# A two-layer encoder on one core: the opening stage in a new order, with its own ring for the modulation weights

## The chip, the cores and the metric

The kernel runs on one core of a Trainium2 chip. TensorE (PE) multiplies matrices into PSUM, VectorE (DVE), ScalarE (ACT) and GpSimd (POOL) work on elements, SyncE (SP) issues most transfers from HBM; each engine takes its instructions in order and waits on semaphores. The metric is the device time of one execution in microseconds (us), as the median of several runs. Less is better.

## What is computed

```python
for i in range(2):
    shift, scale, gate = split(silu(c) @ w_mod[i] + b_mod[i])      # each D = 1024
    h = rmsnorm(x, norm_g[i]) * (1 + scale) + shift                # x: 512 x 1024
    if i == 0:     # layer A: short convolution
        z, bg, cg, xh = split(h @ a_w_in)                          # each E = 2048
        y = bg * conv3(cg * xh) * silu(z);   y = y @ a_w_out
    else:          # layer B: spatial gating
        z, u, v = split(h @ b_w_in);  u, v = gelu(u), layernorm(gelu(v))
        y = u * (w_s @ v + b_s) * silu(z);   y = y @ b_w_out
    x = x + gate * y
out = rmsnorm(x, final_g)
```

All in fp32. The kernel holds x transposed, 128 channels a tile (8 tiles, KD) by 512 positions.

## The kernel before

To keep fp32 accuracy, every operand of a large product is cut in two: an upper part that ScalarE writes as fp32r (`h_hi`, `w_hi`), and the rest that VectorE subtracts (`h_lo`, `w_lo`). A product is then three matmuls, hi*hi, hi*lo and lo*hi. Layer A works on E = 2048 in eight pairs of 256 columns. Pair 0 is done in the opening in the plain way; pairs 1 to 7 are done in a loop by a scheme with seven products of 256 columns (Q1 to Q7) for each group of weights (four groups a pair, `g` = 0 to 3; `product`, L890 to L892), for which VectorE first makes sums of h (`s_f`, cut into `s_hi` and `s_lo`) and of weights (`wt`, by `t_sums`), lower parts of a weight block (`b11_low`) and of the sums (`t_low`), and ScalarE copies each bank's partial result between products (`copy_p`, L545).

The opening, up to that loop, does this. Eight tiles of x arrive in four transfers and ScalarE squares them; VectorE adds the squares up with GpSimd's help; TensorE sums over channels (L829), GpSimd takes the power -1/2 (L417), and a product with diagonals spreads the result (`p_rstd`, L805, "broadcast"). In parallel the modulation of layer A is needed: shift and scale of h are sums over 1024 rows of `w_mod`, which arrive as 16 slots of 512 KB, s0 to s3, four slots for each pair of h tiles (kp = 0 to 3). VectorE multiplies each 512 columns by silu(c) and adds them up (`start_tile`, L1153 and L1156, 32 steps in all), TensorE sums over partitions with four one-column products (`start_columns`, L774), VectorE makes `amp` and `mod`, and ScalarE makes the two tiles of h and their upper parts (L471, L475). Two of the steps of kp = 0 are done by TensorE from the raw slot with silu(c) as one moving column (`direct_columns`, L819). GpSimd does the scalings of x by the norm for tiles 2 to 7 (L429) and the lower part of every odd h tile (L425). TensorE then has, for each kp, 24 matmuls for cg and xh (L845) and 12 for z (`p_pair`), and at the end 48 for bg.

The order is written out by hand in each engine's block. All slots of the opening, modulation and weights (0 to 7), go through one ring `raw` of four slots in the order of `START_ORDER`; SyncE waits on `consumed`, which VectorE raises when it is done with a slot. `keep_clock` (L767) issues matmuls on constants whose result nobody reads, 15, 3 and 12 of them.

## Time and profile before

| | us |
|---|---|
| median of 3 runs | 846.73 |
| lowest, highest | 845.67, 846.97 |
| profiled execution | 845.46 |
| its span in the trace | 843.4 |
| TensorE busy | 819.3 |
| VectorE busy | 627.2 |
| ScalarE busy | 381.7 |
| GpSimd busy | 52.4 |

The profiled execution is one run with its own time; 2.1 us of it lie outside the span that the trace covers. Times in the trace are microseconds from the start of the span. Busy shares are averages over stages with different limits, so the stretches are to be read one by one. A line number is the line of the kernel before; a helper's line stands for all its calls.

### The profile page before, as it was taken

What the parts mean: (1) busy time and instruction counts of PE and PEld (TensorE: products, weight loads), DVE (VectorE), ACT (ScalarE), POOL (GpSimd) and SP (SyncE); (2) the same over time, 40 slices, a digit from 0 to 9 for tenths busy, and PEclk for the clock granted to TensorE, in tenths of its full rate; (3) what the DMA queues carried; (4) which work ended last, traced back from release to release, by engine and by line L of the source; (5) the groups of instructions that cost most, each with busy time, mean ns of one, the idle gap of its engine ahead of it and who ended that gap; (6) DMA issues with size and microseconds to landing.
All of it is one profiled execution on the core that took longest, in us unless ns stands there. A gap on an engine that the chain in (4) does not pass through costs nothing.

```text
span 843.4 us, 14120 instructions
## 1 busy us (share of the span) xinstructions
PE 819.3 (97%) x5026; PEld 736.7 (87%) x5026; DVE 627.2 (74%) x966; ACT 381.7 (45%) x514; POOL 52.4 (6%) x56
## 2 busy tenths in 40 slices
PE   5899899999999999999999999999999999999996
PEld 4778899999999999987889888888888888888896
DVE  4989989898989999898653664477776667667534
ACT  3346566666665665553323832244344444422210
POOL 2510000001000000000000100000000000000000
PEclk9899999999999999999999999999999999999999
DMA  7674466666565666578422232222222222174203
GB/s 269 231 252 151 125 181 196 182 188 173 175 187 173 187 174 181 177 281 300 158 76 75 76 125 99 99 82 93 99 75 87 87 94 80 50 273 149 78 1 100
DMA packets 35467, 123.13 MB, mean 146 GB/s; under 512 B 3824, under 2 KB 6000, under 8 KB 35440
## 3 DMA queue, kind: packets, MB, share of 16 engines
q1 hardware_dynamic: 31120, 107.05, 35.7%
q0 software_dynamic: 4032, 14.68, 9.2%
q10 hardware_dynamic: 288, 1.05, 0.3%
q8 instruction: 16, 0.26, 0.1%
q14 instruction: 11, 0.09, 0.0%
HBM read 105.99 MB, written 2.10 MB: 128 GB/s over the span
## 4 chain that ended last, share of the span: by engine, by line
PE 88%; DVE 8%; issue 1%; DMA 1%; ACT 1%; SPq 0%; DVEq 0%
PE pp L751 14%; PE pp L753 14%; PE pp L752 14%; PE pp L890 7%; PE pp L891 7%; PE pp L892 7%; PE p_aux L892 4%; PE p_aux L890 4%; PE p_aux L891 4%; PE pp L1026 3%; PE pp L1027 3%; PE pp L1028 3%; DVE acc_s L1153 3%; PE p_aux L1079 1%; DVE w_lo_s L1133 1%
## 5 line engine op out<-in xcount | busy, mean ns | idle before, releaser
L456 ACT ACTIVATE w_hi<-raw 128x1024 fp32r<-128x1024 f32 x77 | 81.5, 1060 | 183.9 <-PE pp L753 117.3
L1133 DVE TENSOR_TENSOR w_lo<-raw,w_hi 128x1024 fp32r<-128x1024 f32 x80 | 97.5, 1222 | 70.4 <-ACT w_hi L456 70.0
L751 PE MATMUL pp<-y_hi,w_hi 128*128 128x512 f32 (+1 forms) x320 | 114.6, 358 | 0.7 <-DVE y_lo L1407 0.4
L752 PE MATMUL pp<-y_lo,w_hi 128*128 128x512 f32 (+1 forms) x320 | 111.1, 347 | 0.0
L753 PE MATMUL pp<-y_hi,w_lo 128*128 128x512 f32 (+1 forms) x320 | 111.1, 347 | 0.0
L751 PE MATMUL pp<-h_hi,w_hi 128*128 128x512 f32 x256 | 100.2, 391 | 0.0
L753 PE MATMUL pp<-h_hi,w_lo 128*128 128x512 f32 x256 | 99.7, 389 | 0.0
L752 PE MATMUL pp<-h_lo,w_hi 128*128 128x512 f32 x256 | 99.6, 389 | 0.0
L891 PE MATMUL pp<-h_lo,wh 128*128 128x256 f32 x280 | 79.2, 283 | 0.0
L892 PE MATMUL pp<-h_hi,wl 128*128 128x256 f32 x280 | 79.2, 283 | 0.0
L890 PE MATMUL pp<-h_hi,wh 128*128 128x256 f32 x280 | 79.2, 283 | 0.0
L751 PEld LDWEIGHTS pp<-y_hi,w_hi 128*128 128x128 f32 x320 | 60.6, 189 | 8.0 <-issue 1.5
L753 PEld LDWEIGHTS pp<-y_hi,w_lo 128*128 128x128 f32 x320 | 60.5, 189 | 7.6
L1347 DVE TENSOR_TENSOR wl<-wt,wh 128x1024 fp32r<-128x1024 f32 x56 | 66.5, 1219 | 0.1
L890 PE MATMUL pp<-s_hi,wh 128*128 128x256 f32 x224 | 63.5, 283 | 2.8 <-ACT pc L545 2.8
L752 PEld LDWEIGHTS pp<-y_lo,w_hi 128*128 128x128 f32 x320 | 60.6, 189 | 6.3
L538 ACT ACTIVATE wh<-wt 128x1024 fp32r<-128x1024 f32 x56 | 59.0, 1054 | 14.4 <-DVE wt L1328 8.4
L891 PE MATMUL pp<-s_lo,wh 128*128 128x256 f32 x224 | 63.4, 283 | 0.0
L892 PE MATMUL pp<-s_hi,wl 128*128 128x256 f32 x224 | 63.4, 283 | 0.0
L892 PE MATMUL p_aux<-s_hi,wl 128*128 128x256 f32 x224 | 63.4, 283 | 0.0
L890 PE MATMUL p_aux<-s_hi,wh 128*128 128x256 f32 x224 | 63.4, 283 | 0.0
L891 PE MATMUL p_aux<-s_lo,wh 128*128 128x256 f32 x224 | 63.4, 283 | 0.0
(187 smaller groups left out, 1918.5 us busy)
## 6 DMA issues: line engine op xcount, KB each, us to landing
raw<-in_stream SPq DMA_DIRECT2D x160, 512.0 KB, 3.4
wl<-raw POOLq DMA_DIRECT2D x28, 512.0 KB, 4.5
raw_l<-in_stream SPq DMA_DIRECT2D x18, 512.0 KB, 4.7
raw_m<-in_stream SPq DMA_DIRECT2D x14, 512.0 KB, 3.3
x_s<-in_xt SPq DMA_DIRECT2D x4, 512.0 KB, 6.6
x<-in_xt SPq DMA_DIRECT2D x4, 512.0 KB, 5.8
out_t<-x SPq DMA_DIRECT2D x8, 256.0 KB, 2.3
rs_bc<-in_wst ACTq DMA_DIRECT2D x1, 512.0 KB, 7.7
```

The lines of the kernel that those rows point to most:

```text
L456: act.activation(to[:, slot[0], :], raw[:, slot[1], :], ACT.Copy).then_inc(hi_cut, 1)
L538: act.activation(wh[g % 2][:, at], wt[g % 2][:, at], ACT.Copy).then_inc(t_hi_cut, 1)
L751: pe.matmul(out, hi, rhs_hi(kt), start=first and n == 0, stop=False)
L752: pe.matmul(out, hi, rhs_lo(kt), start=False, stop=False)
L753: mm = pe.matmul(out, lo, rhs_hi(kt), start=False, stop=last and n == len(kts) - 1)
L890: pe.matmul(out, hi, hi_of(k), start=fresh and k == 0, stop=False, skip_group_check=not fresh)
L891: pe.matmul(out, hi, lo_of(k), start=False, stop=False, skip_group_check=not fresh)
L892: mm = pe.matmul(out, lo, hi_of(k), start=False, stop=k == 3, skip_group_check=not fresh)
L1026: pe.matmul(v_bank(st)[:, :], left_hi, right_hi, start=kt == 0, stop=False)
L1027: pe.matmul(v_bank(st)[:, :], left_hi, right_lo, start=False, stop=False)
L1133: dve.tensor_tensor(lo[:, slot[0], :], raw[:, slot[1], :], f32(hi[:, slot[0], :]), ALU.subtract).then_inc(consumed, 1)
L1347: dve.tensor_tensor(wl[par][:, part], wt[par][:, part], f32(wh[par][:, part]), ALU.subtract).then_inc(t_cut, 1)
```

## The change

The change touches the opening only. What it does:

- The slots s0 to s3 get a ring of their own, `raw_s`, with 12 places; the weights keep the ring of four. SyncE issues all of them in the old order, and waits only for the third set (its places lie over the squares) and for the fourth set (it uses places of s0). The small constants `cols` are issued by ScalarE.
- TensorE takes the first two slots of s0 and the first of s1 straight from the raw slot, six steps of the 32 instead of two. It does so with silu(c) repeated 120 times as the moving operand (`silu_w`), so each product has 120 columns, of which one is read.
- GpSimd no longer adds squares, scales tiles or makes lower parts of h. VectorE does these.
- `keep_clock` is 6 and 2 instead of 15, 3 and 12.
- The order of VectorE, ScalarE and TensorE up to the loop is new; the middle tap of pair 0's convolution goes to ScalarE.

TensorE from its start to the first matmuls of layer A. Before (`ssum` are the sums of squares, `work` the diagonals, `acc_s` the modulation sums):

```order
L767 MATMUL pp<-ones 128x128 x15
L829 MATMUL p_aux<-ones,ssum 128x1 x4
L819 MATMUL p_aux<-silu_c,raw 128x1 x8
L767 MATMUL pp<-ones 128x128 x3
L805 MATMUL p_aux<-work,ones 128x512
L774 MATMUL p_aux<-ones,acc_s 128x1 x4
L767 MATMUL pp<-ones 128x128 x12
L845 MATMUL pp<-h_hi,w_hi_s 128x512 x4
```

and with the change:

```order
L796 MATMUL pp<-ones 128x128 x6
L841 MATMUL p_aux<-silu_w,raw_s 128x120 x8
L854 MATMUL p_aux<-ones,ssum 128x1 x4
L841 MATMUL p_aux<-silu_w,raw_s 128x120 x8
L831 MATMUL p_aux<-ones,acc_s 128x1 x4
L825 MATMUL p_aux<-work,ones 128x512
L841 MATMUL p_aux<-silu_w,raw_s 128x120 x8
L796 MATMUL pp<-ones 128x128 x2
L868 MATMUL pp<-h_hi,w_hi_s 128x512 x4
```

The column sums of kp = 0 now stand ahead of the broadcast, and wide products ahead of the channel sums, between them and the column sums, and ahead of layer A.

VectorE from the last modulation steps of kp = 1. Before (`w_lo_s` lower weights, `amp` and `mod` the modulation, `hf` h before cutting):

```order
L1153 SCALAR_TENSOR_TENSOR acc_s<-raw,silu_c,acc_s 128x512 x6
L1133 TENSOR_TENSOR w_lo_s<-raw,w_hi_s 128x1024
L1276 SCALAR_TENSOR_TENSOR amp<-p_aux,cols 128x2
L1279 TENSOR_TENSOR mod<-p_aux,cols 128x2
L1282 TENSOR_TENSOR amp<-amp,cols 128x2
L1133 TENSOR_TENSOR w_lo_s<-raw,w_hi_s 128x1024
L1156 TENSOR_SCALAR acc_s<-raw,silu_c 128x512
L1240 TENSOR_TENSOR h_lo<-hf,h_hi 128x512
```

and with the change (`raw_s` is the new ring, L1247 the scaling by the norm):

```order
L1256 TENSOR_TENSOR h_lo<-hf,h_hi 128x512
L1174 SCALAR_TENSOR_TENSOR acc_s<-raw_s,silu_c,acc_s 128x512
L1256 TENSOR_TENSOR h_lo<-hf,h_hi 128x512
L1174 SCALAR_TENSOR_TENSOR acc_s<-raw_s,silu_c,acc_s 128x512 x3
L1154 TENSOR_TENSOR w_lo_s<-raw,w_hi_s 128x1024
L1283 SCALAR_TENSOR_TENSOR amp<-p_aux,cols 128x2
L1286 TENSOR_TENSOR mod<-p_aux,cols 128x2
L1289 TENSOR_TENSOR amp<-amp,cols 128x2
L1247 TENSOR_TENSOR hf<-x_s,p_aux 128x512 x2
L1154 TENSOR_TENSOR w_lo_s<-raw,w_hi_s 128x1024
L1256 TENSOR_TENSOR h_lo<-hf,h_hi 128x512
```

Scalings and lower parts of odd tiles stand between what was there, the lower weights of slot 2 before `amp` instead of slot 1.

ScalarE from the copies of cg to the loop. Before (`pc<-pp` L545 is a product's partial result, `wh` from `wt` the upper sums):

```order
L566 ACTIVATE tmp<-pp 128x512 x2
L456 ACTIVATE w_hi_s<-raw 128x1024
L549 ACTIVATE s_hi<-s_f 128x1024 x2
L517 ACTIVATE wh_55<-raw 128x512
L525 ACTIVATE wh_55<-raw 128x1024
L530 ACTIVATE wl_57<-raw 128x1024
L575 ACTIVATE tmp<-p_aux 128x512 x2
L538 ACTIVATE wh_55<-wt_59 128x1024 x2
L517 ACTIVATE wh_56<-raw 128x512
L545 ACTIVATE pc<-pp 128x256
L525 ACTIVATE wh_56<-raw 128x1024
L538 ACTIVATE wh_56<-wt_60 128x1024
L545 ACTIVATE pc<-pp 128x256
L530 ACTIVATE wl_58<-raw 128x1024
L538 ACTIVATE wh_56<-wt_60 128x1024
L545 ACTIVATE pc<-pp 128x256
```

and with the change (there the copy is L560):

```order
L581 ACTIVATE tmp<-pp 128x512 x2
L472 ACTIVATE w_hi_s<-raw 128x1024
L532 ACTIVATE wh_57<-raw 128x512
L540 ACTIVATE wh_57<-raw 128x1024
L545 ACTIVATE wl_59<-raw 128x1024
L553 ACTIVATE wh_57<-wt_61 128x1024 x2
L590 ACTIVATE work<-tmp,cols 128x512 x2
L564 ACTIVATE s_hi<-s_f 128x1024
L595 ACTIVATE tmp<-p_aux 128x512 x2
L564 ACTIVATE s_hi<-s_f 128x1024
L532 ACTIVATE wh_58<-raw 128x512
L560 ACTIVATE pc<-pp 128x256
L540 ACTIVATE wh_58<-raw 128x1024
L545 ACTIVATE wl_60<-raw 128x1024
L560 ACTIVATE pc<-pp 128x256 x2
L553 ACTIVATE wh_58<-wt_62 128x1024 x2
```

Of group 1 the copies of Q6 and Q7 now stand ahead of the cut of the sums (`wh` from `wt`), and the two SiLU of z (`tmp<-p_aux`) behind the third cut of s.

The diff, cut to what the text speaks of:

```diff
-SQ_START = 5
-DIRECT = (3, 5)
-WARM = (15, 3, 12)
+SQ_START = 7
+WARM = (6, 2)
+S_RING = 12
+S_DIRECT = (2, 1, 0, 0)
+WIDE = 120
+WIDE_AT = 32
...
+        raw_s = at_kb("raw_s", 92, [P, S_RING, SLOT])
+        silu_w = at_kb("silu_w", 188, [P, KD, WIDE])
...
         def _(sp):
-            sp.dma_start(cols[:, :], cols_d[:, :]).then_inc(cols_in, 16)
             for k in range(4):
                 sp.dma_start(x_s[:, 2 * k:2 * k + 2, :], xt[:, 2 * k:2 * k + 2, :]).then_inc(x_in[k], 16)
-            for q in range(RING):
-                sp.dma_start(raw[:, q, :], stream[q, :, :]).then_inc(landed[q], 16)
-            with sp.Fori(1, Q_RING // RING) as r:
-                for j in range(RING):
-                    sp.wait_ge(consumed, RING * r + (j - RING + 1))
-                    sp.dma_start(raw[:, j, :], stream[RING * r + j, :, :]).then_inc(landed[j], 16)
+            for q, what in enumerate(START_ORDER[:Q_RING]):
+                if isinstance(what, str):
+                    kp, j = int(what[1]), START_ORDER[:q].count(what)
+                    slot = s_at(kp, j)[0]
+                    if kp == 2:
+                        sp.wait_ge(sq_added, SQ_START)
+                    if kp == 3:
+                        if j < S_DIRECT[0]:
+                            sp.wait_ge(direct_done, j + 1)
+                        else:
+                            sp.wait_ge(s_used, j + 1 - S_DIRECT[0])
+                    sp.dma_start(raw_s[:, slot, :], stream[q, :, :]).then_inc(ms_in[slot], 16)
+                else:
+                    n = CUT_ORDER.index(what)
+                    if n >= RING:
+                        sp.wait_ge(consumed, n - 3)
+                    sp.dma_start(raw[:, n % RING, :], stream[q, :, :]).then_inc(landed[n % RING], 16)
...
         def _(pool):
-            for n, k in enumerate((3, 5)):
-                ...
-                pool.tensor_tensor(work[:, 0, :], work[:, 0, :] if n else x_squared(1), x_squared(k),
-                                   ALU.add).then_inc(sq_odd, 1)
...
-                    for kp in range(1, DPAIRS + 2):
-                        if kp > 1:
-                            kt = 2 * kp - 3
-                            pool.tensor_tensor(h_lo[:, kt, :], hf[:, kt, :], h_hi[:, kt, :].bitcast(F32),
-                                               ALU.subtract).then_inc(h_cut, 1)
-                        for kt in (2 * kp, 2 * kp + 1):
-                            if kt < KD:
-                                pool.tensor_tensor(hf[:, kt, :], x_s[:, kt, :], work[:, 1, :],
-                                                   ALU.mult).then_inc(h_scaled, 1)
...
+            act.dma_start(cols[:, :], cols_d[:, :]).then_inc(cols_in, 16)
             act.wait_ge(cols_in, 16)
             act.activation(silu_c[:, :], cols[:, C_C:C_C + KD], ACT.Silu).then_inc(sc_ready, 1)
...
+            def direct_columns(kp, j):
+                slot, land = s_at(kp, j)
+                pe.wait_ge(ms_in[slot], land)
+                for n in range(2):
                     for t in range(4):
+                        mm = pe.matmul(p_small[:, WIDE_AT + WIDE * t:WIDE_AT + WIDE * (t + 1)],
+                                       raw_s[:, slot, S * n + P * t:S * n + P * (t + 1)], silu_w[:, 2 * j + n, :],
+                                       start=j == 0 and n == 0 and t == 0, stop=False, skip_group_check=True)
+                mm.then_inc(direct_done, 1)

             pe.wait_ge(consts, 3)
-            pe.wait_ge(sq_ready, 3)
+            pe.wait_ge(sq_ready, 1)
             keep_clock(WARM[0])
+            pe.wait_ge(wide_ready, 1)
+            direct_columns(0, 0)
             pe.wait_ge(sq_added, SQ_START)
             for st in range(NCH):
                 mm = pe.matmul(p_rstd[:, st:st + 1], ssum[:, P * st:P * (st + 1)], ones[:, 0:1], start=True, stop=True)
             mm.then_inc(stat_sum, 1)
-            pe.wait_ge(sc_ready, 1)
-            direct_columns()
-            keep_clock(WARM[1])
-            broadcast(p_rstd[:, :], 2, ALL)
-            start_columns(0)
-            keep_clock(WARM[2])
+            direct_columns(0, 1)
+            start_columns(0)
+            broadcast(p_rstd[:, :], 2, ALL)
+            pe.wait_ge(amp_ready, 1)
+            direct_columns(1, 0)
+            keep_clock(WARM[1])
...
-                if kp < 3:
-                    start_columns(kp + 1)
+                if kp == 0:
+                    start_columns(1)
...
+                    if u == 0 and kp in (1, 2):
+                        start_columns(kp + 1)
...
+            dve.wait_ge(sc_ready, 1)
+            dve.tensor_copy(silu_w[:, :, :], silu_c[:, :].unsqueeze(2).broadcast_to([P, KD, WIDE])).then_inc(wide_ready, 1)
+            for k in range(1, KD):
                 dve.wait_ge(sq_ready, k + 1)
...
+            start_amp(1)
+            scale_pair(1, p_rstd[:, :], ALL, 0)
+            cut_lo_start(1)
+            cut_h_tile(0, 2, ALL)
+            start_tiles(2, 0)
+            cut_h_tile(0, 3, ALL)
+            start_tiles(2, 1, 2, 3, 4, 5, 6, 7)
+            scale_pair(2, p_rstd[:, :], ALL, 0)
...
-            s_low(1)
-            cut_lo_start(7)
             t_sums(1, 0)
             b11_low(1, 0)
+            t_low(1, 0, 0)
+            s_low(1)
+            t_low(1, 0, 1)
+            s_sum_at(2)
             n = []
             for u in range(2):
-                w = cols[:, C_CONV + KE + u:C_CONV + KE + u + 1]
-                n.append(step(dve.tensor_scalar(work[:, u, :], tmp[:, 2 + u, :], w, None, ALU.mult)))
-            n = [conv_tap(0, u, 2, conv_tap(0, u, 0, n[u])) for u in range(2)]
-            t_low(1, 0, 0)
-            t_low(1, 0, 1)
-            s_low(2)
+                dve.wait_ge(conv_first, u + 1)
+                n.append(conv_tap(0, u, 2, conv_tap(0, u, 0)))
+                if u == 0:
+                    s_low(2)
```

## Rows read from the trace of the kernel before

**Rows 1.** The page, part 1: busy us, share of the span, instructions
```profile
PE 819.3 (97%) x5026; PEld 736.7 (87%) x5026; DVE 627.2 (74%) x966; ACT 381.7 (45%) x514; POOL 52.4 (6%) x56
```

**Rows 2.** Busy time by stretch: us, PE, PEld, DVE, ACT, POOL, PEclk, DMA, GB/s
```profile
26.00:34.00 8.00, 5.66 (x27) 4.33 (x25) 7.68 (x8) 2.12 (x2) 5.07 (x3) 1.00 0.47 148
76.00:88.00 12.00, 9.53 (x65) 8.70 (x63) 11.86 (x15) 3.03 (x5) 0.00 (x0) 1.00 0.50 147
100.00:140.00 40.00, 40.00 (x336) 40.00 (x336) 35.97 (x51) 24.55 (x36) 3.12 (x5) 1.00 0.61 175
```

**Rows 3.** Waits of PE from 26 to 140 us: total, times, longest
```profile
PE p_aux L774 <- DVE acc_s L1153: 3.3, 2, 2.3
PE pp L890 <- ACT pc L545: 2.8, 1, 2.8
```

**Rows 4.** Timeline, 61 to 92 us, of DVE, then ACT, then PE: start, us, engine
```profile
61.21 1.47 DVE L1133 TENSOR_TENSOR w_lo_s<-raw,w_hi_s 128x1024 fp32r<-128x1024 f32 x1 [1.63 <-ACT w_hi_s L456]
...
75.05 0.88 DVE L1439 TENSOR_SCALAR work<-tmp,cols 128x512 f32<-128x512 f32 x2
...
88.27 0.69 DVE L1341 TENSOR_TENSOR wl<-raw,wh 128x512 fp32r<-128x512 f32 x1
...
86.93 1.06 ACT L538 ACTIVATE wh<-wt 128x1024 fp32r<-128x1024 f32 x1 [4.34 <-DVE wt L1328]
87.89 0.37 ACT L545 ACTIVATE pc<-pp 128x256 f32<-128x256 f32 x1
...
91.29 0.28 PE L890 MATMUL p_aux<-h_hi,wh 128*128 128x256 f32 x1
```

**Rows 5.** Groups of DVE by line and shape, 8 to 62 us: busy us, mean ns
```profile
L1153 DVE SCALAR_TENSOR_TENSOR acc_s<-raw,silu_c,acc_s 128x512 f32<-128x512 f32 x26 | 27.0, 1037 | 1.3
```

**Rows 6.** The chain that ended last, in order of time: start, us, what
```profile
24.29 1.64 DVE acc_s L1153
...
32.40 0.76 DVE acc_s L1153
...
33.94 1.13 DVE w_lo_s L1133
...
57.38 0.83 ACT hf L471
58.23 0.63 ACT h_hi L475
```

**Rows 7.** The same groups, of POOL, 8 to 62 us
```profile
L429 POOL TENSOR_TENSOR hf<-x_s,work 128x512 f32<-128x512 f32 x6 | 10.5, 1770 | 4.4 <-ACT work L494 4.4
```

**Rows 8.** Timeline of all engines, 9 to 32 us
```profile
9.21 2.41 ACT L482 ACTIVATE x_sq<-x_s 128x512 f32<-128x512 f32 x4 [0.16 <-DMA x_s<-in_xt]
...
14.55 1.05 PE L829 MATMUL p_aux<-ones,ssum 128*128 128x1 f32 x8 [0.73 <-DVE ssum L1254]
...
18.19 1.55 PE L805 MATMUL p_aux<-work,ones 128*128 128x512 f32 x2
...
19.77 1.28 DVE L1231 TENSOR_TENSOR hf<-x_s,p_aux 128x512 f32<-128x512 f32 x2 [0.45 <-PE p_aux L805]
...
21.10 5.06 PE L767 MATMUL pp<-ones 128*128 128x128 f32 x24
...
25.92 1.18 PE L845 MATMUL pp<-h_hi,w_hi_s 128*128 128x512 f32 x4
...
31.04 0.39 PE L845 MATMUL pp<-h_hi,w_lo_s 128*128 128x512 f32 x1
```

**Rows 9.** DMA issues: the constants at 0.76 us, the first slot at 3.09 us
```profile
cols<-in_cols SPq DMA_DIRECT2D x1, 80.0 KB, 1.9
...
raw<-in_stream SPq DMA_DIRECT2D x1, 512.0 KB, 8.6
```

**Rows 10.** Busy time by stretch, as rows 2
```profile
10.00:11.00 1.00, 1.00 (x7) 1.00 (x6) 1.00 (x1) 0.89 (x2) 0.86 (x2) 1.00 1.03 422
20.00:25.00 5.00, 5.00 (x24) 5.00 (x25) 4.71 (x8) 3.38 (x5) 3.23 (x2) 0.50 0.80 286
```

More of the change, by code:

```diff
@@ L219, in build @@
         sq_ready = sem("sq_ready")
-        sq_odd = sem("sq_odd")
+        ms_in, s_used, wide_ready = [sem(f"ms_in{j}") for j in range(S_RING)], sem("s_used"), sem("wide_ready")
+        conv_first = sem("conv_first")
         direct_done = sem("direct_done")
@@ L572, in _ @@
             neg_b2(1, 0)
+            hi_t(1, 0, 0, first=True)
+            hi_t(1, 0, 1, first=True)
+            for u in range(2):
+                act.wait_ge(xh_used, u + 1)
+                act.activation(work[:, u, :], tmp[:, 2 + u, :], ACT.Copy,
+                               scale=cols[:, C_CONV + KE + u:C_CONV + KE + u + 1]).then_inc(conv_first, 1)
+            hi_s(2)
             for u in range(2):
@@ L767, in keep_clock @@
                     pe.matmul(pp[3][:, 0:P], ones[:, :], ones[:, :], start=True, stop=True)
-            def mod_columns(pairs, used, begun=False, of=consumed):
-                pe.wait_ge(of, used)
-                for col, parts in pairs:
-                    for n, part in enumerate(parts):
-                        mm = pe.matmul(p_small[:, col:col + 1], part, ones[:, 0:1], start=n == 0 and not begun,
-                                       stop=n == len(parts) - 1, skip_group_check=begun)
-                mm.then_inc(acc_used, 1)
             def column(layer, j, n):
@@ L849, in _ @@
                     k = 2 * kp + n
-                    if k == 0:
-                        pe.wait_ge(h_hi_cut, 1)
-                        for s in (w_hi_s, w_lo_s):
-                            for b in range(2):
-                                for u in range(2):
-                                    part(b, u, n, s, h_hi, s is w_hi_s, False)
+                    pe.wait_ge(h_hi_cut, k + 1)
+                    for s in (w_hi_s, w_lo_s):
+                        for b in range(2):
+                            for u in range(2):
+                                part(b, u, n, s, h_hi, s is w_hi_s and k == 0, False)
                     pe.wait_ge(h_cut, k + 1)
@@ L1453, in _, with beside_0 @@
             s_low(3)
-            def beside_0(i, first=False):
-                t_sums(i, 1, first)
+            def beside_0(i):
+                t_sums(i, 1)
                 b11_low(i, 1)
-                if not first:
+                if isinstance(i, int) and i == 1:
+                    c_22(i, 0)
+                else:
                     c_12(i, -1)
```

221 lines of the change are left out of this document (112 added, 109 removed).

## The prediction

> **What bounds the kernel now.** The page first: TensorE is busy 97% of the span [rows 1]. Then the busy time by stretch: from 100 to 140 us TensorE is busy for all 40.00 us, while VectorE has 4 us to spare; from 26 to 34 and from 76 to 88 it is the other way round, VectorE busy nearly throughout and TensorE idle for 2.3 and 2.5 us [rows 2]. The waits of TensorE say for whom: between 26 and 140 us, 3.3 us for the modulation sums and 2.8 us for a copy of ScalarE's [rows 3]. So after about 91 us the time is a fixed amount of matmul work, and what the opening is worth is read at one point: where product Q1 of the loop's second group begins, at 91.29 us [rows 4]. Everything behind it moves with it. The profiled execution took 845.46 us, 1.27 below the median of 846.73; I make the sum on the profile and put the saving on the median.
>
> **Why VectorE is slow there.** A modulation step (L1153) takes 0.76 us on its own but 1.64 us where GpSimd runs beside it, and the mean of all 26 is 1037 ns [rows 5, 6]. 26 times (1.037 - 0.76) is 7.2 us that GpSimd's six scalings of 1770 ns [rows 7] and its other passes cost VectorE. The change gives GpSimd's work to VectorE: six scalings, four lower parts, two additions of squares more, 12 x 0.64 (two scalings take 1.28 us [rows 8]) = 7.7 us. Of the 32 modulation steps six go to TensorE where two did before, 4 x 0.76 = 3.0 us, and two conv products, 0.88 us together [rows 4], go to ScalarE. Net: 7.2 + 3.0 + 0.9 - 7.7 = 3.4 us less VectorE time. The rest of the gain has to come from waits, so I follow the chain.
>
> **Up to the first product of layer A.** The squares end where they did (9.21 + 2.41 = 11.6 us [rows 8], bound by x), the seven additions on VectorE follow at 0.7 us each and end near 12.5. But TensorE, in order, now has eight matmuls of 120 columns ahead of the sums: they wait for the first modulation slot, which landed at 3.09 + 8.6 = 11.7 [rows 9]. At half clock a keep-clock matmul of 128 columns costs 5.06 / 12 = 0.42 us [rows 8], so these cost 0.40 each, 3.2 us, and end at 14.8; no row shows such a wide fp32 product, and at full clock it would be half. The sums take 1.1 and end at 15.9 (before: 15.60). Power, diagonals and broadcast follow as before: 18.19 - 15.60 = 2.6 us from the end of the sums to the broadcast [rows 8], so it could start at 18.5. Now the column sums of pair 0 stand ahead of it, so 18.7, and it ends at 20.2 (1.55 us, before 19.74). Then VectorE scales two tiles (1.28) and makes the lower weights (1.13 [rows 6]): 22.7. TensorE does eight wide products and two keep-clock ones until 23.3, which is where the first product starts, against 25.92 before [rows 8], when twelve keep-clock matmuls stood ahead of it. **Term 1: 2.6 us.** Weights and slots are not late: at 422 GB/s [rows 10] 512 KB take 1.25 us, so behind the first at 11.7 the four slots of pair 1 (with one of w between) are there by 21.7, and nothing waits for a ring that VectorE must free.
>
> **The four pairs.** A pair's 24 products take 5.5 us (25.92 to 31.4 [rows 8]) and its two p_pair units, 12 products, 2.7. Pair 0: 23.3 + 5.4 = 28.7; columns of pair 1 until 29.7 (its tiles have been summed since 28.2); amp 0.4, a scaling 0.63, h 0.83 and its upper part about 0.6 [rows 6]: 32.3. TensorE, with 12 products meanwhile, starts pair 1 at 32.7. Pair 1 ends at 38.1; half its unit; VectorE has summed the eight tiles of pair 2 (0.44 + 7 x 0.76, behind two scalings, w_lo and two lower parts) at 39.7, columns until 40.7, amp behind the scalings 41.3, h 42.8: pair 2 starts at 42.9. In the same way the tiles of pair 3 end at 50.6 (TensorE waits 1.0), pair 3 starts at 53.8, its second h is ready at 55.1, w_hi of slot 6 at 56.1. VectorE's w_lo of slot 6 starts at 56.1, against 61.21 before [rows 4]. **Terms 1 and 2 together: 5.1 us.** TensorE idles at most 1.0 us at a time there.
>
> **From there to the loop.** Before, VectorE needed 88.27 + 0.61 - 61.21 = 27.7 us from that w_lo to the lower part b11 of group 1. The new order has the same work without the two conv products (-0.9), plus 0.7 us of waits where VectorE gets to things sooner than ScalarE: 27.5, so 83.6. Product Q1 of group 1 wants exactly that. Before, it began 2.4 us after it (91.29 - 88.88), because Q7 stood still: the copy of Q6 ran at 87.89 behind the cut of the sums that VectorE had only just made at 86.93 [rows 3, 4]. The new order copies first. **Term 3: 2.4 + 0.2 us.** A new wait appears: TensorE ends its last unit at 73.4 but the two SiLU of z now stand behind s_hi 2, which needs the fourth s sum (72.8); Q1 of group 0 begins at 74.95, 1.5 us idle. It costs nothing, because group 1 waits for VectorE anyway; without that cover it would cost its 1.5 us. VectorE then goes into the loop 2.5 us behind TensorE instead of 0.4, but with 4 us to spare in 40 [rows 2], and b11 of group 2 would be there 3.8 us early.
>
> **Sum.** Q1 of group 1 at 83.7 instead of 91.29: 7.6 us. I take off 0.6 for some twelve hand-overs between engines at 0.05 us more than I counted: 7.0 us. 845.46 - 7.0 = 838.5 for a profile like this one; **839.7 us** on the median. About 0.2% (1.7 us) is what a measurement of this kernel can tell from no change.
>
> **Which way the clock falls** is the largest unknown. The granted clock was 0.50, the level of 1.2 GHz, from 20 to 25 us, after one-column products between 14.5 and 17.2 and only three keep-clock matmuls [rows 8, 10]; it rose again during the twelve keep-clock matmuls. I took half clock for the first wide block, full for the second, half for the broadcast and part of the third. Rival A, half clock all through: broadcast at 21.8, first product at 26.4, and the whole chain 3.1 us later: 842.8. Above it, full clock from the first block on: first product at 22.1, 1.1 us earlier: 838.6. For A speaks that 22 dummy matmuls go and thin columns stay; against it, that 24 wide ones come in their place. The Trainium skill ("TensorE: Matmul & The Clock Gate", Part 1) says that the same kernel shows different counts of slow matmuls from run to run, since the watch is not tied to the kernel's start; by it both cases could stand among the runs, and no row of one execution can show that.
>
> **Rival B: VectorE stays slow.** If the long steps are not GpSimd's doing but the transfers' or ScalarE's, each of the remaining steps keeps 1.04 us; the chain then reaches Q1 of group 1 at 89.7, a gain of 1.0: 845.7. Against it: steps before 33 us and after it are 1.64 and 0.76 us under the same stream of transfers, and only GpSimd differs [rows 6].
>
> **Rival C, the slower side: the constants come late.** The transfer of cols is issued by ScalarE on a queue of its own beside SyncE's now unbroken row of x and 11 slots, and ScalarE's SiLU, then all eight squares stand behind it. Landing up to about 8 us it costs nothing (TensorE's wide block covers it); after that every us is one us. At 15 us it has eaten the 7.0, from there the kernel is slower; at 18 it is 849.7. Before, it landed 1.9 us after its issue, ahead of everything. For C: the first slot, in the row behind x, took 8.6 us to land [rows 9]. Against it: that one has 512 KB and 2 MB ahead of it in its queue, cols has 80 KB and nothing ahead of it. The Trainium skill ("DMA: Bandwidth & Descriptors", Queues, rings and completion order) has each DMA engine take turns between queues, by which cols would be through in 2 to 4 us and C would be out of the question; no row of before has two queues at work in the opening.
>
> **Rival D: given back in the loop.** VectorE's larger lag could make TensorE stop in groups 1 and 2 (t sums late, or the GpSimd accumulation of b2 late). It can give back what TensorE gained over VectorE, 7.6 - 1.9 = 5 us at most: 844.7.
>
> **How the numbers follow.** Forecast 0.50, full clock sooner 0.10, A 0.20, B 0.06, D 0.06, C 0.05, something else 0.03. The range holds forecast, both clocks and the near part of D: from 838.6 less the 0.6 of hand-overs and 1 us for spread between runs, 837.0, to 844.0. Faster by over 0.2%: 0.50 + 0.10 + 0.20 + most of D = 0.85; within 0.2%: B and a part of C, 0.09; slower 0.06.
>
> **What would show it.** Steps of L1174 all near 0.76 us; the first product at 23 to 27 us; waits for modulation sums of at most 1 us; w_lo of slot 6 at 56 to 60; no wait of TensorE for a copy before Q7; a new wait for SiLU of about 1.5 us; Q1 of group 1 at 84 to 87, and then the same 40 us of matmuls in 40. It is wrong if those steps stay above 1 us, if squares begin after 8 us, or if the stretch after 100 us shows TensorE idle.

## The result and the profile after

| | before | after |
|---|---|---|
| median, us (runs) | 846.46 (4) | 836.45 (4) |
| lowest, highest | 845.67, 846.97 | 835.64, 838.89 |
| profiled execution | 845.46 | 836.55 |
| its span | 843.4 | 834.7 |

The ratio is 0.9887, 95% interval 0.9865 to 0.9909: 10 us faster. The forecast was 839.7 with a range of 837.0 to 844.0. The direction is right; the time lies 0.55 us below the range, and none of the named cases gave so short a time.

The views are those of before, now of the changed kernel. The page, part 1 (against [rows 1]):

```profile
PE 814.7 (98%) x5014; PEld 732.8 (88%) x5014; DVE 621.5 (74%) x973; ACT 381.7 (46%) x515; POOL 33.5 (4%) x44
```

Busy time by stretch, with the columns of [rows 2]:

```profile
26.00:34.00 8.00, 8.00 (x39) 6.51 (x38) 7.42 (x14) 3.74 (x5) 0.00 (x0) 1.00 1.03 409
76.00:88.00 12.00, 12.00 (x102) 12.00 (x101) 11.70 (x16) 6.52 (x11) 0.86 (x1) 1.00 0.48 132
100.00:140.00 40.00, 40.00 (x336) 40.00 (x335) 37.23 (x53) 24.78 (x37) 3.44 (x4) 1.00 0.68 198
```

Both stretches in which TensorE stood idle for 2.3 and 2.5 us are full now, and the loop still is. The waits of TensorE from 26 to 140 us (against [rows 3]):

```profile
PE pp L911 <- ACT tmp L595: 1.4, 1, 1.4
PE pp L868 <- ACT h_hi L491: 1.2, 2, 0.6
PE p_aux L831 <- DVE acc_s L1174: 1.1, 2, 0.7
PE pp L780 <- DVE tmp L1462: 0.3, 1, 0.3
```

The wait for a copy is gone, the waits for modulation sums are 0.7 at most, and the foretold wait for SiLU is there. VectorE's groups from 5 to 62 us (against [rows 5]) show the steps at the pace that they have alone:

```profile
L1174 DVE SCALAR_TENSOR_TENSOR acc_s<-raw_s,silu_c,acc_s 128x512 f32<-128x512 f32 x22 | 16.5, 749 | 0.9
```

TensorE's timeline up to layer A:

```profile
6.29 2.90 PE L796 MATMUL pp<-ones 128*128 128x128 f32 x12 [6.29 <-ACT x_sq L499]
10.63 3.74 PE L841 MATMUL p_aux<-silu_w,raw_s 128*128 128x120 f32 x16 [1.44 <-DMA raw_s<-in_stream]
14.16 1.12 PE L854 MATMUL p_aux<-ones,ssum 128*128 128x1 f32 x8
15.14 2.02 PE L841 MATMUL p_aux<-silu_w,raw_s 128*128 128x120 f32 x16
...
17.91 1.10 PE L825 MATMUL p_aux<-work,ones 128*128 128x512 f32 x2
18.85 1.94 PE L841 MATMUL p_aux<-silu_w,raw_s 128*128 128x120 f32 x16
...
21.52 1.21 PE L868 MATMUL pp<-h_hi,w_hi_s 128*128 128x512 f32 x4 [0.28 <-DVE w_lo_s L1154]
...
27.13 0.95 PE L831 MATMUL p_aux<-ones,acc_s 128*128 128x1 f32 x8
```

The first block of wide products took 3.74 us and the next two 2.02 and 1.94: half pace, then full pace up to layer A. (The granted-clock column reads 1.00 throughout here, the slow first block included. In this stretch the durations tell the pace, the column does not.) Last, from the timelines near the loop, two rows of VectorE, then Q1 of group 0 and Q1 of group 1 on TensorE (against [rows 4]):

```profile
54.75 1.23 DVE L1154 TENSOR_TENSOR w_lo_s<-raw,w_hi_s 128x1024 fp32r<-128x1024 f32 x1 [0.26 <-ACT w_hi_s L472]
...
81.58 0.69 DVE L1373 TENSOR_TENSOR wl<-raw,wh 128x512 fp32r<-128x512 f32 x1
...
73.91 0.38 PE L911 MATMUL pp<-h_hi,wh 128*128 128x256 f32 x1 [1.37 <-ACT tmp L595]
...
82.64 0.28 PE L911 MATMUL p_aux<-h_hi,wh 128*128 128x256 f32 x1
```

Product Q1 of group 1 begins at 82.64 us, against 91.29: 8.65 us, and the spans differ by 8.7. So all of it came before that point and nothing was given back behind it.

### The profile page after: what moved, and what is told of

It reads as the page before. It is cut to its first block, busy times and chain, and to the rows that moved or that the text cites. A ratio compares the mean times of both kernels' runs of the same rounds, so it can differ in the third digit from the quotient of the medians.

```text
span 834.7 us, 14019 instructions
## 1 busy us (share of the span) xinstructions
PE 814.7 (98%) x5014; PEld 732.8 (88%) x5014; DVE 621.5 (74%) x973; ACT 381.7 (46%) x515; POOL 33.5 (4%) x44
## 4 chain that ended last, share of the span: by engine, by line
PE 91%; DVE 5%; ACT 1%; issue 1%; DMA 1%; SPq 0%; DVEq 0%; ACTq 0%
PE pp L780 15%; PE pp L781 14%; PE pp L782 14%; PE pp L911 7%; PE pp L912 7%; PE pp L913 7%; PE p_aux L913 4%; PE p_aux L912 4%; PE p_aux L911 4%; PE pp L1047 3%; PE pp L1048 3%; PE pp L1049 3%; PE p_aux L1100 1%; DVE acc_s L1174 1%; DMA raw_s<-in_stream 1%
```

## The experiments

All are medians of device time; each chip ran the kernel before beside them (847.2 to 847.9 us there), and the changed kernel once more gave 836.61, so the ratio to before is the fair comparison between chips; a difference "to the change" is against its 836.45. "Start" is the first product of layer A. One more figure helps: the time of the profiled execution less its start. It is 836.55 - 21.52 = 815.03 us in the change, and says what was lost behind the start, whatever the start was.

### Does the clock follow from the wide products? (thin)

The changed kernel with one moving column again:

```diff
-                        mm = pe.matmul(p_small[:, WIDE_AT + WIDE * t:WIDE_AT + WIDE * (t + 1)],
-                                       raw_s[:, slot, S * n + P * t:S * n + P * (t + 1)], silu_w[:, 2 * j + n, :],
+                        mm = pe.matmul(p_small[:, WIDE_AT + WIDE * t:WIDE_AT + WIDE * t + 1],
+                                       raw_s[:, slot, S * n + P * t:S * n + P * (t + 1)], silu_w[:, 2 * j + n, 0:1],
```

> The changed kernel with one moving column instead of 120 in the three blocks that TensorE takes from the raw slots; nothing else differs. Theory W (the wide products hold TensorE's clock through the opening): the granted clock falls to half somewhere between 15 and 23 us, the broadcast takes 1.55 instead of 1.10 us, the first pair's 24 products run partly at 0.43 us each; the time rises by 1.5 to 5 us against the changed kernel's 836.5, so 838 to 841.5. Theory N (the clock is held by the rest, or is not on the path in the opening): the blocks get shorter by 1 us each, the sums of squares start 1 us sooner, and the time is 835 to 837.

Measured: 843.81 us (842.63 to 844.71), ratio 0.9961 (0.9946 to 0.9976), 7.4 us slower than the change and above the 841.5 that theory W allowed. Its busy time by stretch, columns as above:

```profile
10.00:13.00 3.00, 2.14 (x20) 2.17 (x20) 2.08 (x4) 0.63 (x2) 0.00 (x0) 1.00 1.03 419
13.00:20.00 7.00, 7.00 (x31) 6.54 (x32) 3.68 (x10) 1.64 (x3) 1.51 (x1) 0.51 1.03 409
20.00:30.00 10.00, 10.00 (x34) 8.36 (x33) 8.66 (x12) 4.67 (x6) 0.00 (x0) 0.50 1.03 408
```

and TensorE's timeline in it, the first two blocks that were wide, the first products of layer A, the column sums of pair 1:

```profile
10.86 1.92 PE L841 MATMUL p_aux<-silu_w,raw_s 128*128 128x1 f32 x16 [1.44 <-DMA raw_s<-in_stream]
...
13.95 3.55 PE L841 MATMUL p_aux<-silu_w,raw_s 128*128 128x1 f32 x16
...
25.04 2.05 PE L868 MATMUL pp<-h_hi,w_hi_s 128*128 128x512 f32 x4
...
32.97 0.94 PE L831 MATMUL p_aux<-ones,acc_s 128*128 128x1 f32 x8
```

TensorE counts as busy without a gap from 13 to 30 us and yet the granted clock falls to 0.50, the level of 1.2 GHz, after the one-column products, and stays there through half of pair 0. The column sums of pair 1 are 5.8 us late (32.97 against 27.13), and the profiled execution is 6.1 us longer than the change's: 3.5 of it the later start (25.04), 2.6 behind the start, where half of pair 0 ran at half pace. The other executions took up to 2.1 us more than the profiled one (842.6 to 844.7); no trace shows where. This is rival A of the prediction with one difference: the start was earlier than its 26.4, but the pace of layer A itself suffered, which A did not price.

### Would keep-clock products do as well? (thin_keep, b_warm0, warm00)

thin_keep is thin with `WARM = (6, 14)`, b_warm0 the kernel before with `WARM = (15, 3, 0)`, warm00 the changed kernel with `WARM = (0, 2)`.

> The changed kernel with one moving column and, to bring the clock back, 14 keep-clock products of 128 columns in place of 2 ahead of layer A, as the kernel before had 12. Theory: the twelve more cost 5.0 us at half clock, after which the clock is full, while with one column and 2 of them pair 0 lost 5.4 us to half clock: it comes out within 1.5 us of that kernel, 843 to 845, well above the wide one's 836.5, so the wide columns win because they do needed work while they hold the clock. Rival: the clock comes back after a few of them and pair 0 is quick: 840 or less.

Measured: 846.81 (843.44 to 847.25), ratio 0.9986 (0.9974 to 0.9997). Against thin it is 3 us slower, not within 1.5. TensorE's timeline in it:

```profile
25.99 4.79 PE L796 MATMUL pp<-ones 128*128 128x128 f32 x28
30.54 1.17 PE L868 MATMUL pp<-h_hi,w_hi_s 128*128 128x512 f32 x4
...
36.11 0.94 PE L831 MATMUL p_aux<-ones,acc_s 128*128 128x1 f32 x8
```

Pair 0 starts 5.5 us later than in thin and takes 5.57 us instead of 7.93: 5.5 lost, 2.4 won. Not all of the 5.5 belongs to the added products. In this execution the first block already ran at half pace (3.55 us, against 1.92 in thin's), and the broadcast began 1.8 us later (20.87 against 19.07); the other 3.7 us are the fourteen products instead of two. So the two profiles alone would put the keep-clock products 1.3 us behind, and the rest of the 3 us is how the clock stood. My 5.4 for pair 0 was wrong, since only half of its products were slow in thin. Behind the start this execution took 815.12 us, as the change did: once pair 0 runs at full pace, everything that separates the two is the start, 30.54 against 21.52. The wide columns win because they hold the clock with work that was needed anyway.

> The kernel before without the twelve keep-clock matmuls ahead of the first product. Theory V (VectorE sets the pace of the opening, TensorE's late start at 25.9 us costs nothing): the first product starts near 23 us, at half clock, its 24 products take up to 10 us, end near 33 us, where TensorE waited for VectorE anyway until 34; time within 1 us of before. Theory K (the clock of the opening is on the path): pair 0 ends after 34 us and the half clock lasts into pair 1, and the time rises by 2 to 5 us.

Measured: 847.01 (844.7 to 849.45), ratio 1.0002 (0.9989 to 1.0015). From 17 to 30 us the granted clock was 0.52 where it was 0.74 before, and in the median it cost nothing. The start was at 24.67 us, not near 23, since TensorE waited 2.1 us for h; later it waited 2.6 us for modulation sums at 35 instead of 2.3 at 34. In the kernel before VectorE set the pace there, so its clock was worth nothing; in the changed kernel it is worth 7 us (thin).

> No keep-clock products at all ahead of the first wide block. Theory: the wide products alone bring the clock up; the first block runs at half clock (3.5 to 3.7 us) as it did with six of them in the profile looked at, and the second may do so too; first layer-A product at 21.5 to 23.5, median 836.5 to 838.5. Rival: without them the clock comes up a block or two later, the broadcast and the third block are slow as well, first product at 24 or later, 839 or more.

Measured: 839.27 (836.68 to 842.1), ratio 0.9912 (0.989 to 0.9933). The execution that was profiled, 836.68, starts at 21.57 just like the change, with the same 3.74 us in its first block: in these two executions the six keep-clock products made no difference. Four of the other five took 2.4 to 5.4 us more; where, no trace shows.

### Is the slow VectorE GpSimd's doing? (b_dve_h, pool_busy)

b_dve_h is the kernel before with GpSimd's six scalings and four lower parts on VectorE (the two additions of squares stay):

```diff
-                            pool.tensor_tensor(h_lo[:, kt, :], hf[:, kt, :], h_hi[:, kt, :].bitcast(F32),
-                                               ALU.subtract).then_inc(h_cut, 1)
...
-                                pool.tensor_tensor(hf[:, kt, :], x_s[:, kt, :], work[:, 1, :],
-                                                   ALU.mult).then_inc(h_scaled, 1)
...
+                if kp:
+                    scale_pair(kp, p_rstd[:, :], ALL, 0)
...
+                cut_h_tile(0, 2 * kp + 1, ALL)
```

> The kernel before, with GpSimd's six scalings of h and four lower parts given to VectorE (the squares stay, and so do ring, order, one-column products and keep-clock matmuls); ScalarE's copy of the broadcast goes. Theory V (GpSimd's passes made VectorE's slow): the modulation steps take 0.75 us in the mean instead of 1.04, VectorE wins 7.2 us and has 6.4 more to do, so the time falls by about 1, 845 to 847 beside 846.5. Rival (the slow steps come from the transfers in flight): the steps keep 1.0 us, and the time rises by 5 to 7 us.

Measured: 844.44 (841.09 to 845.52), ratio 0.9966 (0.995 to 0.9982). VectorE's steps among its groups from 8 to 62 us:

```profile
L1139 DVE SCALAR_TENSOR_TENSOR acc_s<-raw,silu_c,acc_s 128x512 f32<-128x512 f32 x26 | 19.5, 749 | 0.9
```

and TensorE's waits from 26 to 140 us:

```profile
PE pp L876 <- ACT pc L531: 2.8, 1, 2.8
PE pp L831 <- DVE h_lo L1226: 2.6, 3, 1.0
```

The mean falls from 1037 to 749 ns: the contention is GpSimd's (rival B falls). The gain, 2.7 us, is more than the 1 us expected. The wait for modulation sums is gone; one for lower parts takes its place, and the copy still stops TensorE. In the profiled execution the granted clock was 0.50 from 17 to 26 us and the start was at 27.04. That with VectorE out of the way the clock begins to count is a reading that b_both below fits (it started at 23.47), but no run tests it apart.

pool_busy turns it round: the changed kernel with six GpSimd products of 128x512 on constants into a spare tile, two after each scaling of tiles 1, 3 and 5.

```diff
+                    for n, (tile, ops) in enumerate(((1, 2), (3, 2), (5, 2))):
+                        pool.wait_ge(h_scaled, tile + 1)
+                        for _ in range(ops):
...
+                            pool.tensor_tensor(spare[:, :].rearrange("p (a e) -> p a e", e=P),
+                                               ones[:, :].unsqueeze(1).broadcast_to([P, 4, P]),
+                                               ident[:, :].unsqueeze(1).broadcast_to([P, 4, P]),
+                                               ALU.mult).then_inc(spared, 1)
```

> The changed kernel with six extra multiplications of 128x512 on GpSimd, two after each of the scalings of tiles 1, 3 and 5, on constants and a spare tile that nobody reads. Theory V: each takes 1.3 to 1.8 us, and VectorE's passes with two inputs in SBUF beside them take about twice their time, so VectorE loses 3 to 6 us, and the time rises by as much less the 1 us of waits that it has: 2 to 5 us, so 838.5 to 841.5. Rival (no contention): no change, modulation steps at 0.75 us throughout.

Measured: 842.02 (841.29 to 846.82), ratio 0.9949 (0.993 to 0.9967), 5.5 us more than the change for 10.9 us of GpSimd work, and above the range expected. Behind the start (20.61) it lost 6.1 us. VectorE beside a pair of them, from 19.50 to 23.14 us:

```profile
19.34 1.22 DVE L1165 TENSOR_TENSOR w_lo_s<-raw,w_hi_s 128x1024 fp32r<-128x1024 f32 x1
20.47 1.52 DVE L1188 TENSOR_SCALAR acc_s<-raw_s,silu_c 128x512 f32<-128x512 f32 x1
22.03 1.66 DVE L1185 SCALAR_TENSOR_TENSOR acc_s<-raw_s,silu_c,acc_s 128x512 f32<-128x512 f32 x1
```

0.48 and 0.75 us became 1.52 and 1.66, while the lower part that had begun 0.16 us before GpSimd kept its 1.22. The Trainium skill ("SBUF — State Buffer", SBUF: two separate sides) calls the port pair that the two engines share an exclusive lock, taken by a GpSimd pass, or by a VectorE pass with two inputs in SBUF or in a two-port mode, and held for the whole instruction by whoever starts first. The trace agrees for the passes with two inputs, down to the one that had begun first; whether the one-input pass (L1188) is in such a mode no run shows.

### The closing: the copy, the SiLU, VectorE's row (copy_late, b_copy, b_both, silu, early_t)

copy_late is the changed kernel with the old closing order, b_copy the kernel before with the new one, b_both b_dve_h with the new one. ScalarE's part of it (VectorE's second gate sum, `c_22`, also moves, to right behind `b11_low`):

```diff
...
+            copy_p(1, 0, 0)
+            hi_b2(1, 1, first=True)
+            neg_b2(1, 1)
+            copy_p(1, 0, 1)
+            copy_p(1, 0, 2)
+            hi_t(1, 1, 0, first=True)
+            hi_t(1, 1, 1, first=True)
...
```

> The changed kernel with the old closing order of ScalarE and VectorE for group 1: the copies of Q6 and Q7 behind the cuts of the sums, and VectorE's second gate sum behind the lower sums. Theory T (the third term of the prediction, 2.4 us, is the copy standing behind the cut): TensorE stands still again before Q7, for about 2.5 us, and the time rises by 2 to 3 us: 838.5 to 839.5. Rival (the stall was only the lateness of VectorE, which is less late now): under 1 us more, 836.5 to 837.5.

Measured: 839.64 (838.2 to 843.08), ratio 0.9919 (0.9898 to 0.994). TensorE's waits from 26 to 140 us, the first two:

```profile
PE pp L911 <- ACT pc L560: 1.7, 1, 1.7
PE pp L911 <- ACT tmp L595: 1.4, 1, 1.4
```

The stall before Q7 is back, at 1.7 us instead of the 2.5 expected. From the lower part of slot 6 (54.40) to Q1 of group 1 (84.24) it took 29.84 us, 1.95 more than in the change, and behind the start (21.17) it lost 2.2. The 3.2 us between the medians are more than that; the six executions scatter over 4.9 us.

> The kernel before with nothing changed but the closing order: ScalarE copies Q6 and Q7 of group 0 ahead of the cuts of t, and VectorE adds the first partial result right behind b11_low. Theory (term 3 stands alone, since the copy is the wait that ends last there): TensorE no longer waits 2.8 us for a copy, Q1 of group 1 begins right behind b11_low, 1.7 to 2.5 us earlier: 844.9 to 845.7 where the kernel before has 847.3. Rival: without the copy in its way TensorE only meets the cuts of t in Q5 to Q7 of group 1, and nothing is won.

Measured: 843.98 (843.35 to 845.99), ratio 0.9961 (0.9946 to 0.9976): 3.6 us in the medians, more than expected. From the lower part of slot 6 to Q1 of group 1 the profiled execution took 27.89 us (62.49 to 90.38) against 30.08 before, 2.2 us, as expected; where the other 1.4 us of the medians come from, this one profile does not show. Among TensorE's waits in the same stretch the one for the copy became one of 0.6 for VectorE:

```profile
PE p_aux L781 <- DVE acc_s L1160: 2.5, 1, 2.5
PE p_aux L897 <- DVE wl L1348: 0.6, 1, 0.6
```

> The same closing order on the kernel before with GpSimd's scalings and lower parts on VectorE (which alone gave 2.7 us). Theory: the two add up, since one shortens VectorE's row up to the loop and the other what follows it: 4.4 to 5.2 us, 842.2 to 843.0. The remaining 5 to 6 us of the change then belong to the wide direct steps, the ring and the order before pair 0. Rival: GpSimd's share moves the end of VectorE's row so far ahead that TensorE sets the pace in the closing, and the copy gives less than 1 us more: above 843.5.

Measured: 839.45 (839.0 to 840.72), ratio 0.9912 (0.9897 to 0.9927). 8.1 us, where the two parts alone gave 2.7 and 3.6. The sum rule failed by 1.8 us; in its profile pair 0 starts at 23.47 against 27.04 in b_dve_h, and the 12 keep-clock products ahead of it took 2.92 us instead of 4.74, so part of it is the execution's clock. Two edits of the old kernel thus bring three quarters of the change (0.9912 against 0.988).

silu moves ScalarE's two SiLU of z to right behind `neg_b2(1, 0)`; early_t adds to that, on VectorE, the sums and lower parts of group 1 ahead of `silu_mul` and y.

> The changed kernel with ScalarE's two SiLU of z moved ahead of the upper parts of group 0's sums, where ScalarE is idle for 1.15 us, instead of behind the third cut of s. Theory P (TensorE arrives at Q1 of group 1 just when VectorE is ready, so the wait of 1.4 us for SiLU is only partly covered): TensorE enters the loop 1.4 us sooner, waits for VectorE about 0.9 us ahead of Q1 of group 1, and the time falls by 0.3 to 0.5 us: 836.0. Theory C (as in the prediction, the wait is wholly covered): no difference below 0.1 us. Theory L (nothing else is behind): 1.4 us less, 835.1.

Measured: 836.23 (835.52 to 838.48), ratio 0.9869 (0.985 to 0.9888), 0.2 to 0.4 us below the change's two medians, within their scatter. Behind the start (23.53) its profiled execution took 814.95 us against 815.03, so the order itself is worth about 0.1 us: theory C, not P. TensorE's wait moved on to VectorE (view of waits, 26 to 140 us):

```profile
PE p_aux L911 <- DVE wl L1373: 1.3, 1, 1.3
```

> As the run with SiLU moved, and VectorE also makes the sums, lower block and lower sums of group 1 ahead of pair 0's last two gate products and y. Theory P: both what TensorE waits for at the loop's start is gone, Q1 of group 1 begins about 81.2 instead of 82.64, and the time falls by 1.0 to 1.4 us: 835.2. Rival: y, now 5 us later, or the first sums of the loop's step, some 1.5 us later on VectorE, make TensorE wait instead (Q5 of group 1 wants y), and the time is 836 to 837.

Measured: 837.07 (835.97 to 841.86), ratio 0.9895 (0.9872 to 0.9918), no gain: the rival was right. What left the first place came back in the next, by the same view:

```profile
PE pp L911 <- DVE tmp L1390: 0.8, 1, 0.8
PE pp L911 <- DVE y L1493: 0.5, 1, 0.5
```

### The ring (ring4)

`S_RING = 4` in the changed kernel, so that a modulation slot again waits for one to be used.

> The changed kernel with a ring of 4 instead of 12 places for the modulation slots; weights keep their own. Theory R (the deep ring is needed, since at 1.25 us a slot and VectorE at 1.5 us a slot the stream must run ahead): the slots of pair 1 land some 4 us after TensorE and VectorE free those of pair 0, near 20 to 24 us, VectorE waits for each first slot and the time rises by 3 to 6 us. Theory F (as in the prediction, what the slots need is never late, 3 us a slot are wanted in the mean): within 1.5 us.

Measured: 839.61 (838.85 to 841.37), ratio 0.9916 (0.9899 to 0.9933), 3.2 us slower than the change. The size is as theory R had it, the place is not: nothing waited for the slots of pair 1 near 20 to 24 us. Up to 43 us it runs like the change; then weight slot 5, queued behind modulation slots that must wait for their places, is late, and VectorE with it (its timeline):

```profile
46.55 1.23 DVE L1153 TENSOR_TENSOR w_lo_s<-raw,w_hi_s 128x1024 fp32r<-128x1024 f32 x1 [2.22 <-ACT w_hi_s L471]
```

### Why executions differ, and a faster version (after_again, warm9, warm9_silu)

The changed kernel once more, and with `WARM = (9, 2)`, so that TensorE has work until the first slot lands at 10.6 us; warm9_silu has silu's order too.

> The changed kernel once more, unaltered, beside the next three on one chip. Theory: its executions differ by where the granted clock stands in the first two wide blocks (first layer-A product at 21.5 in the profile looked at, 20.7 and 23.5 in two kernels with the same opening), so a second profile may show another start than 21.5; the median should be 836.0 to 837.5 us. Rival: the start is fixed by the order and shows 21.5 again within 0.2 us; same median.

Measured: 836.61 (836.27 to 838.75), ratio 0.988 (0.9863 to 0.9897), the start at 21.48. The profile alone looks like the rival; but the kernels silu and early_t, with the same opening, started at 23.53 and 20.70 in theirs, with the second block at 3.49 us in one and the first at 2.02 in the other. The first block in silu, then in early_t:

```profile
10.66 3.74 PE L841 MATMUL p_aux<-silu_w,raw_s 128*128 128x120 f32 x16 [1.44 <-DMA raw_s<-in_stream]
...
10.73 2.02 PE L841 MATMUL p_aux<-silu_w,raw_s 128*128 128x120 f32 x16 [1.45 <-DMA raw_s<-in_stream]
```

The Trainium skill ("TensorE: Matmul & The Clock Gate", Part 1) says that the same kernel shows different counts of slow matmuls from run to run; these traces, with one and the same opening, agree.

> Nine keep-clock products in place of six, so that TensorE stays busy from 6.3 us to the first slot's landing at 10.6 instead of standing still for 1.44 us. Theory (that pause is why the first wide block ran at half clock and why executions differ): full clock from the first block in every execution, block 2.0 us instead of 3.7, first layer-A product at 20.5 to 21; but from there VectorE's chain (scalings, modulation sums of pair 1) decides, so the median gains 0.3 to 1.2 us: 835.2 to 836.2. Rival 1 (nothing hangs on the block: the channel sums wait for VectorE's additions until 13 us anyway): within 0.3 us of the unaltered kernel. Rival 2 (the clock comes back only by what follows): block still 3.5 us or more, 836.5.

Measured: 835.65 (835.50 to 835.71), ratio 0.9862 (0.9844 to 0.9879).

> The nine keep-clock products and, on ScalarE, the two SiLU of z ahead of the cuts of t. Theory: the SiLU wait (1.37 us before Q1 of group 0) is about 0.45 us too long for VectorE's cover, and the first block's clock is worth up to 0.8: 834.8 to 836.0, the fastest of the set. Rival: VectorE's b11_low of group 1 sets Q1 of group 1 whatever TensorE does, so it is within 0.4 us of the unaltered kernel.

Measured: 835.65 (835.24 to 835.70), ratio 0.9861 (0.9843 to 0.9878). TensorE's timeline in warm9:

```profile
6.30 4.18 PE L796 MATMUL pp<-ones 128*128 128x128 f32 x18 [6.30 <-ACT x_sq L499]
10.64 2.75 PE L841 MATMUL p_aux<-silu_w,raw_s 128*128 128x120 f32 x16 [0.16 <-DMA raw_s<-in_stream]
...
20.60 1.20 PE L868 MATMUL pp<-h_hi,w_hi_s 128*128 128x512 f32 x4 [0.28 <-DVE w_lo_s L1154]
```

and the first wide block in warm9_silu:

```profile
10.71 2.02 PE L841 MATMUL p_aux<-silu_w,raw_s 128*128 128x120 f32 x16 [0.28 <-DMA raw_s<-in_stream]
```

The start is 0.9 us earlier than in after_again and all of it reaches the end (835.65 for 836.57 in the profiled executions; behind the start both took 815.0 to 815.1). The median is in the range expected, the reason only in part. Full pace from the first block, 2.0 us, came in warm9_silu; in warm9 the block took 2.75. And the pause of 1.44 us does not decide the pace alone: early_t had it and ran its first block at full pace. Nor does the start come any earlier for a quick first block: with 2.02 us TensorE then waits 0.7 us for VectorE's modulation sums, and the start is at 20.66 (warm9_silu) and 20.70 (early_t), against 20.60 with 2.75.

The scatter seems to change more than the median. The highest of four executions with nine products is 0.2 us above the lowest, in warm9_silu 0.5. With six and the same opening it is 3.3 in the change, 2.5 in after_again, 3.0 in silu and 5.9 in early_t, with none 5.4. But five of those 19 executions with six products took over 838 us, so eight in a row below it can still be chance. The SiLU order adds nothing in the median. Beside the change on the same chip, all eight executions lie below all five of it (835.24 to 835.71 against 836.27 to 838.75); the intervals of the ratios overlap.

## Why the prediction was right, and where it was wrong

The direction was right, and so were the mechanisms but for the clock; the size was not, 10 us where 7.0 was forecast. Two steps failed. The first is term 1: 2.6 us were forecast for the start of layer A, and it came 4.4 us earlier. The second is the one that put the saving on the median of before, 1.27 us above the profiled execution. Three of the signs that the prediction named were passed on the early side: the start before 23, the lower part of slot 6 before 56, Q1 of group 1 before 84.

**What bounds the kernel: right.** Q1 of group 1 moved by 8.65 us and the span by 8.7.

**Why VectorE was slow: right**, shown from both sides (b_dve_h, pool_busy). The estimate of 3.4 us less VectorE time was low: the page has 621.5 for 627.2, 5.7 less. The sum did not use it.

**Term 1 (start at 23.3 instead of 25.92): too small by 1.8 us.** It began at 21.52. Three steps of it were off. The first slot was taken to land at 11.7 as before; it landed at 10.6, and the squares ended at 10.4 instead of 11.6, 1.1 us earlier. SyncE issued this slot 0.4 us sooner, since the constants had left its row; the other 0.7 us stay open. It differs between executions too: ring4, with the same order up to there, had the first slot at 11.6. Against that, the first wide block took 3.5 us instead of 3.1, so it ended at 14.16, not 14.8. The 0.42 us for a keep-clock product "at half clock" was 5.06 / 12 over a stretch in which the clock rose; at half pace throughout six of them took 2.90 us, 0.48 each. The last 1.1 us is the clock. I took "half for the broadcast and part of the third". The broadcast took 1.10 us, not 1.55: 0.4 us. The third block ran at full pace, so that TensorE was done 0.3 us before VectorE's lower weights, on which the start then hung; the prediction had TensorE end last, 0.6 us behind them. The step carried the half clock of before, 0.50 from 20 to 25 us, into an opening that had mostly wide products; thin shows what these weigh.

**The clock's rivals were the right question.** The case that happened is none of the three: half pace in the first block, as in the forecast, but full pace in all that followed. Rival A, "half clock all through", stood at 842.8; thin, where it came about, took 843.81. A had the start too late (26.4 for 25.04) and left out that half of pair 0 ran slow as well, 2.3 us. "Full clock from the first block on" is what early_t's profile shows, with the start at 20.70 and not 22.1.

**Terms 1 and 2 (5.1 us): 6.46**, w_lo of slot 6 at 54.75. From the first product to it I had 32.8 us and it took 33.2: the pairs were followed rightly, and TensorE's waits there were at most 0.7 us each. ring4 shows that the 12-place ring is a condition for that.

**Term 3 and the closing (2.6 us): 2.2 in the profile** (30.08 to 27.89 us). copy_late and b_copy confirm the mechanism: by the same measure the copy's place is worth 1.95 and 2.2 us. (The prediction took 0.61 us for b11 where the row has 0.69; nothing hangs on it.)

**The SiLU wait: foretold at 1.5, measured 1.37, "wholly covered" almost.** In silu and b_copy Q1 of group 1 begins 0.13 to 0.14 us after VectorE's b11 is done; in the change 0.37 (81.58 + 0.69 = 82.27, then 82.64). So some 0.24 us showed at that point; at the end silu's profile had 0.1 of it left.

**Sum.** Of the 3.3 us between forecast and median, 1.05 are the chain (8.65 for 7.6: 1.8 more at the start, 0.4 less in the pairs, 0.3 less in the closing), 0.6 the allowance for hand-overs, which was not needed, 0.26 what lies outside Q1 (the profiled executions differ by 8.91), 0.1 the distance of the change's median below its profiled execution, and 1.27 the step from the profile to the median. That step failed because it took the distance of one execution from its median as a property of both kernels. Before scattered over 844.6 to 850.1 us in the 37 runs beside the first eight experiments, the mean granted clock between 0.995 and 0.987; the change's profiled execution lay at its own median. The range ended at 837.0 because it allowed 0.6 and 1 us below the best clock case, but nothing for this.

**Rivals C and D fell.** The constants landed 4.4 us after their issue, a little above the 2 to 4 us that the prediction worked out, and before SiLU at 5.42 us; from 100 to 140 us TensorE was busy for all 40.

**What the parts are worth** depends on where they are tried. Undone in the changed kernel, wide columns cost 7.4, the ring 3.2, the closing order 3.2, and 10.9 us of work given to GpSimd again 5.5. That is more than the 10 us together, so the parts cannot be added up: each is worth more beside the others. Added to the old kernel, two of them gave 8.1. The profile of b_both took 815.53 us behind its start, 0.5 more than the change, and started 1.95 us later, so most of the last 2.9 us is the start. How much of it is wide columns and how much the rest of the opening's order was not measured.

## What to carry to other kernels

Ask first which engine sets the pace: the same clock was worth nothing while VectorE was late (b_warm0) and 7 us once it was not (thin). Where TensorE has to do small fp32 work in an opening, try repeated columns before dummy products ahead of the real ones (836.5 against 846.8 us here); look at the spread of runs as well as at the median to see whether the start is safe. Subtract the start from the time of an execution before crediting an edit behind it. And do not carry one execution's distance from its median into a forecast.

## What the runs showed of the hardware that was not expected

- One-column fp32 products keep TensorE busy in the record but not its clock: in thin it fell to 0.50 at 13 us and stayed there until 30, where 120 columns at the same places left it at full pace in the change.
- Nor did they raise it: in thin_keep the blocks of one column ran at half pace from 10.6 to 26 us (3.55, 3.55 and 3.41 us), busy throughout, while in the change the pace was full behind one wide block.
- At full pace 16 passes of one column took 1.92 us and of 120 columns 2.02: the repeated columns were nearly free.
- GpSimd on constants of its own delays VectorE's one-input pass as well as its two-input one (0.48 to 1.52 us, 0.75 to 1.66).
- The granted-clock column shows 1.00 from the start of a trace even where products go at half pace (3.74 us for what takes 2.02); in thin_keep it does so over the whole opening.
- With pair 0 at full pace, the profiled time less the start was 815.0 to 815.1 us in the change, after_again, warm00, warm9, warm9_silu and thin_keep, with starts from 20.60 to 30.54.
